# The order in which the sync queue requests an expert block's weight rows: down rows ahead of the next block's gate and up rows

## The reference, cut to what matters

```python
def expert_block(xs):
    tok, g, e = xs
    xb = x_pad[tok]                                                # 128 rows of 1024
    hb = jax.nn.silu(xb @ w_exp_gate[e]) * (xb @ w_exp_up[e])      # 1024 x 256 each
    return (hb @ w_exp_down[e]) * g[:, None]                       # 256 x 1024
```

## Time and profile before

| | |
|---|---|
| median of 3 runs | 2122.57 us (2118.84 to 2122.72) |
| the profiled execution | 2121.66 us |
| its span, first to last instruction | 2119.9 us |
| mean granted TensorE clock | 0.932 of full |
| PE busy | 1873.4 us, 88% |
| DVE busy | 1319.6 us, 62% |
| ACT busy | 1032.6 us, 49% |
| POOL busy | 661.7 us, 31% |
| DMA moved | 373.39 MB, mean 176 GB/s |

### The profile page before, as it was taken

The page is one execution under the profiler, slowest core; times in us unless marked ns, Lnnn a source line. Parts: engine busy times, 40 slices in busy tenths (PEclk is TensorE's granted clock), DMA queues, the critical chain, the costliest instruction groups (busy, mean ns, idle before and its releaser), DMA issues. The chain is left out here.

```text
span 2119.9 us, 28187 instructions
## 1 busy us (share of the span) xinstructions
PE 1873.4 (88%) x8590; PEld 1454.6 (69%) x8590; DVE 1319.6 (62%) x1551; ACT 1032.6 (49%) x1348; POOL 661.7 (31%) x507
## 2 busy tenths in 40 slices
PE   7898899996979999999999930789898978998999
PEld 3774567775768888888888820556665557887887
DVE  4673564445769999999999938265556653333322
ACT  3312344432358888888888822255465522222221
POOL 1896990000015666666666610011110100000000
PEclk9998999997789999999999965899999989999999
DMA  8754542123179999999999934332210013331222
GB/s 294 187 161 146 143 125 76 51 78 127 33 258 353 368 381 358 373 374 372 366 359 355 360 114 181 87 82 52 55 50 21 21 50 100 99 119 55 89 95 79
DMA packets 167747, 373.39 MB, mean 176 GB/s; under 512 B 40038, under 2 KB 77350, under 8 KB 159222
## 3 DMA queue, kind: packets, MB, share of 16 engines
q1 hardware_dynamic: 149670, 329.80, 45.3%
q0 software_dynamic: 18000, 42.58, 6.2%
HBM read 356.19 MB, written 29.23 MB: 182 GB/s over the span
## 5 line engine op out<-in xcount | busy, mean ns | idle before, releaser
L108 DVE TENSOR_TENSOR exp_parts<-exp_raw,exp_parts 128x2048 fp32r<-128x2048 f32 x194 | 439.3, 2291 | 57.5 <-ACT exp_parts L1961 52.5
L102 PE MATMUL ps<-exp_parts,xgT 128*128 128x512 f32 x1536 | 377.0, 401 | 7.5 <-DVE xgT L108 4.1
L1961 ACT CAST exp_parts<-exp_raw 128x2048 fp32r<-128x2048 f32 x194 | 368.9, 1917 | 14.9 <-PE ps L102 13.2
L102 PEld LDWEIGHTS ps<-exp_parts,xgT 128*128 128x128 f32 x1536 | 286.3, 190 | 77.3 <-issue 12.7
L102 PE MATMUL ps<-exp_parts,exp_hT 128*128 128x512 f32 x768 | 196.4, 405 | 2.7 <-DVE exp_hT L108 2.7
L102 PE MATMUL ps<-w_down_parts,hidden_parts 128*128 128x512 f32 x768 | 176.4, 392 | 7.1 <-DVE w_down_parts L108 7.1
L102 PE MATMUL ps<-h4T,w_up_parts 128*128 128x512 f32 x768 | 175.7, 391 | 5.5 <-DVE w_up_parts L108 5.5
L1856 POOL DMA_INDIRECT xg<-h_rows,row_index x63 | 145.6, 2311 | 111.2 <-issue 92.0
L102 PEld LDWEIGHTS ps<-w_down_parts,hidden_parts 128*128 128x128 f32 x768 | 145.6, 190 | 37.9 <-issue 7.5
L102 PEld LDWEIGHTS ps<-h4T,w_up_parts 128*128 128x128 f32 x768 | 145.0, 189 | 35.9 <-ACT w_up_parts L156 5.7
L102 PE MATMUL ps<-h3T,w_parts 128*128 128x512 f32 (+1 forms) x576 | 157.2, 427 | 11.9 <-DVE w_parts L108 11.9
(11 more groups left out here) (429 smaller groups left out, 3179.9 us busy)
## 6 DMA issues: line engine op xcount, KB each, us to landing
exp_raw<-in_w_exp_gate SPq DMA_DIRECT2D x130, 512.0 KB
exp_raw<-in_w_exp_up SPq DMA_DIRECT2D x130, 512.0 KB
exp_raw<-in_w_exp_down SPq DMA_DIRECT2D x64, 1024.0 KB
w_up_raw<-in_w_up SPq DMA_DIRECT2D x15, 1024.0 KB, 5.1
w_down_raw<-in_w_down SPq DMA_DIRECT2D x15, 1024.0 KB, 5.2
yk<-y_rows SPq DMA_DIRECT2D x8, 1536.0 KB, 17.1
w_raw<-in_w_in SPq DMA_DIRECT2D x42, 256.0 KB, 3.3
gate_cols<-in_w_mod POOLq DMA_DIRECT2D x18, 512.0 KB
```

The source lines that it names most:

```text
L102: mm = nc.tensor.matmul(out, left[a], right[b], start=start and i == 0, stop=stop and i == 2)
L108: return nc.vector.tensor_tensor(dst, x, high.bitcast(F32), ALU.subtract)
L1961: nc.scalar.copy(dst, src).then_inc(s_hi[kind], 1)
```

## The change

The calls of `gate_up` and `down` trade places in SP's program, in the peeled steps and in the loop. No instruction of another engine is different, and no wait has another value.

```diff
             def body(b, u, first, i):
                 if first:
+                    if u >= 3:
+                        down(b - 1, u - 1, True)
                     if u >= 2:
                         gate_up(b, u, True)
-                    if u >= 3:
-                        down(b - 1, u - 1, True)
                     return
                 with sp.If(b < used + 1):
+                    down(b - 1, u - 1, True)
                     gate_up(b, u, True)
-                    down(b - 1, u - 1, True)
             steps(sp, body, used, 1)
```

## The result

| | before | changed |
|---|---|---|
| median | 2122.64 us (2118.84 to 2123.78, 4 runs) | 2222.26 us (2214.32 to 2237.01, 4 runs) |
| ratio, with its 95% interval | | 1.048 (1.042 to 1.054) |
| profiled execution, span | 2119.9 us | 2214.4 us |
| step of the expert loop, steps 2 to 63 | 9.69 us | 11.32 us |

What follows compares the result with a forecast made beforehand. PE was taken as nearly full, DVE close behind, DMA engines with very little over. B landing half a microsecond late adds 0.22 us a step, 13.6 us over 61 steps: 2121.7 + 13.6 = 2135.3, median 2136 us, range 2120 to 2162.

Steps and rivals of the forecast that it cites:

- Where the loss is: Expert loop: clustered requests, steps of 9.9 us, waits on ACT, DVE and PE; nothing gained or lost outside 603 to 1240 us.
- The ring: SP's request, B's landing, cast, DVE's work, SP's next request but one: S + 10.1 us, 19.8 us over two steps.
- fixed part: Part of the two-step loop after B's landing: B's cast, hand-over to DVE, low B to SP's next request; 8.66 us.
- Request to first packet: Start of each burst: time from SP's request for C until the first data packet moves, taken as 1.0 us.
- Transfer S: Each step's burst: time from its first packet to the last of B, taken as 9.70 us from the loop's rate.
- The stretch at the start of the stage: 9.5 us at the expert stage's start, at 330 GB/s; that rate gives 10.7 us for a whole block.
- a rival with a chance of 0.13: Later burst in the loop: transfer takes 10.7 us, 10.4 us a step, 43 us more, 2166 us; chance 0.13.
- the 13.6 forecast: Loss over 61 loop steps: 9.91 us a step against 9.69, 0.22 us more each, 13.6 us in all.
- The clock: Rival: late weights make gaps on PE in 30 steps, its clock falls, 40 us on top, 2176 us; chance 0.02.
- "A and C are not" late: In the loop A lands 7.9 us after C's request, its cast at 8.3; C lands first and is used last.
- The rule of the Trainium skill: About 2.0 us fixed plus bytes at 436 GB/s: the burst lands after some 10.1 us, in time, at zero cost.
- the case of no change: Rival: the burst lands inside its spare time, the loop stays at 9.69 us a step, 2122.6 us; chance 0.24.

Runs made afterwards that it cites:

- wait_a_c_b: Changed kernel with SP still waiting for C of block b-3 ahead of all requests, but asking in the order A, C, B: 2220.1 us, ratio 1.047 to the kernel before.

## Why the prediction was wrong

- **Where the loss is.** Right: inside the loop alone, with the five requests in a cluster, DMA share under 1 around it, ACT waiting for up rows, DVE for ACT, PE for DVE.
- **The ring.** Right as a mechanism. Its fixed part measured 8.8 us (6.57 from low B to low C, 0.22 to SP, 1.97 for the cast and hand-over) against 8.66.
- **"Request to first packet: ... I take 1.0 us."** Nearly right. C's first packet starts 1.16 us after SP's request on average, and 0.96 us in the nine bursts that find no B of the block before under way.
- **"Transfer S ... I take" 9.70 us.** This is the step that failed: the term was mis-sized by 2.2 us, and they are nearly the whole of the 2.2 us by which B landed later than forecast. From the same starting point S measured 11.9 us. I took the loop's share of 1 and 366 GB/s over to a state in which the engines are not full: over the burst the share was 0.93 and the rate 325 GB/s. And I counted one burst by itself, while 49 of 58 reach into the next. A goes slower than B, but it did so in the kernel before too, so the 9.70 us had this in them. The stretch at the start of the stage, 330 GB/s, was the better row. I set it aside as a ramp and kept it for a rival with a chance of 0.13 and a time of 2166, still 56 us short.
- Together 2.2 us of landing, 1.1 us a step, 67 us over 61 steps, on top of the 13.6 forecast (0.22 x 61 is 13.4). The fixed part is 3 us more, and 16 us are under "The clock" below.
- **"A and C are not" late.** Wrong for A. It lands 9.9 us after C's request, and its cast was at 8.3. Even asked for 7.8 us later with its old landing time it would have been late, by 0.6 or 0.7 us. It costs nothing of its own, as wait_a_c_b shows.
- **The clock.** I gave it 0.02 as a case of its own. It came as a part of this one. The measured step is 0.27 us over the ring, 16 us in all, and 0.15 us when PE was filled, so something like half of it goes with PE's slow groups. The other half was not separated.
- **The rule of the Trainium skill** (DMA: Bandwidth & Descriptors, Anatomy of one DMA: 2.0 us and the bytes at 436 GB/s). The page gives it as a fit for one DMA issued by GpSimd, and the prediction put it on a burst of five from SP. By the estimate from it B would land after some 10.1 us; the trace has 13.35, so the case of no change was further off than mine.
- **What I could have seen.** Time from request to cast (14.5 to 14.75 us) is not spare time. The landing records give it: 7.2 us for A, 6.2 for B, and at times only 4.1. The page of the kernel before prints no landing for these requests, and I filled the gap with a rate. They would have shown A late as well as B, but by 0.6 to 0.7 us each, and so would not have given the 100 us either.

## What to carry to other kernels

A queue of requests that are each issued when their buffer comes free should ask in the order in which the buffers come free: one wait for the latest of them at the head makes all others as late as it. To judge such a move, take the time from landing to use, not from request to use. And do not carry the rate of an evenly loaded queue over to bursts: here the engines were 93% busy in a burst and not 100%, each burst reached into the next, and a piece landed up to 2.3 us later after its own request than before. If the consumer's work also frees the buffer, the delay comes back as a ring, and each microsecond of landing costs half of one in every step where two buffers are in turn.

## What the runs showed of the hardware that I had not expected

- Matrices read in two passes, first one 4 KB of every 8 KB and then the other: the first pass moved at 221 to 289 GB/s with a DMA share of 0.93 to 0.99, the second alone at 377 GB/s. The same bytes in whole rows of 8 KB moved at 391. Why is open.
- DMAs into 64 partitions each brought all data to 234 GB/s at a share of 0.99 (700 to 1200 us). The same whole rows by one DMA over 128 partitions moved at 337 GB/s at a share of 0.91.
- A share of 1 is therefore no measure of rate: it stood between 0.97 and 1.03 at anything from 221 to 414 GB/s.
